# Layer 0's gate vector and layer 1's conditioning vectors moved from TensorE to GpSimd

## The reference

```
sc = jax.nn.silu(c)
scc = jax.nn.silu(c_ctx)
shift, scale, gate = jnp.split(sc @ mod_w[l] + mod_b[l], 3, axis=-1)
hx = modulate(rmsnorm(x, norm_g[l]), shift[:, None], scale[:, None])
...                                  # layer 0: convolution and two-way recurrence, layer 1: pooled mixer
x = x + gate[:, None] * out_x
```

## Time and profile before

| | |
|---|---|
| median of 3 runs (lowest to highest) | 1827.26 us (1826.8 to 1828.82) |
| profiled execution | 1828.44 us |
| its span in the profile | 1827.1 us |
| TensorE busy | 1749.3 us, 96% of the span |
| VectorE busy | 1059.6 us, 58% |
| ScalarE busy | 758.7 us, 42% |
| GpSimd busy | 18.9 us, 1% |
| mean granted TensorE clock | 0.976 of full speed |

### The profile page before, as it was taken

The page is one execution under the profiler, slowest core; times in us unless marked ns, Lnnn a source line. Parts: engine busy times, 40 slices in busy tenths (PEclk is TensorE's granted clock), DMA queues, the critical chain, the costliest instruction groups (busy, mean ns, idle before and its releaser), DMA issues.

```text
span 1827.1 us, 19870 instructions
## 1 busy us (share of the span) xinstructions
PE 1749.3 (96%) x8054; PEld 1411.2 (77%) x8054; DVE 1059.6 (58%) x1450; ACT 758.7 (42%) x1028; POOL 18.9 (1%) x39
## 2 busy tenths in 40 slices
PE   6899999999999999999889998999989999999996
PEld 4688888888778788888677865776778788888885
DVE  4766799899775756663455353444546644444333
ACT  3587654654442433333333544433433332322221
POOL 0000000000000000000000000000000000000000
PEclk9999999999898999999999998999999999999998
DMA  7344433333323232223222121222122222323321
GB/s 313 118 169 141 159 116 125 129 116 127 120 90 102 81 103 93 92 93 104 91 70 84 55 69 46 67 72 69 65 75 92 92 93 93 102 95 103 101 96 46
DMA packets 49963, 185.81 MB, mean 102 GB/s; under 512 B 5392, under 2 KB 5392, under 8 KB 49616
## 3 DMA queue, kind: packets, MB, share of 16 engines
q1 hardware_dynamic: 42624, 155.21, 25.2%
q0 software_dynamic: 4848, 17.80, 3.0%
q10 hardware_dynamic: 2400, 11.53, 1.6%
HBM read 182.42 MB, written 2.10 MB: 101 GB/s over the span
## 4 chain that ended last, share of the span: by engine, by line
PE 84%; DVE 7%; ACT 6%; issue 2%; ACTq 1%; DMA 0%; DVEq 0%
PE banks L1439 25%; PE banks L1441 24%; PE banks L1440 24%; PE banks L1471 2%; PE banks L1703 2%; ACT w_hi L389 1%; PE banks L1459 1%; PE banks L1452 1%; PE banks L1725 1%; PE banks L1747 1%; PE banks L1793 1%; DVE w_lo L816 1%; DVE u L950 1%; ACTq L415 1%; DVE h_lo L889 1%
## 5 line engine op out<-in xcount | busy, mean ns | idle before, releaser
L1439 PE MATMUL banks<-h_hi,w_hi 128*128 128x512 f32 x1408 | 559.3, 397 | 10.5 <-DVE h_lo L825 5.0
L1441 PE MATMUL banks<-h_hi,w_lo 128*128 128x512 f32 x1408 | 551.8, 392 | 0.0
L1440 PE MATMUL banks<-h_lo,w_hi 128*128 128x512 f32 x1408 | 551.4, 392 | 0.0
L816 DVE TENSOR_TENSOR w_lo<-raw,w_hi 128x1024 fp32r<-128x1024 f32 x292 | 355.4, 1223 | 290.1 <-ACT w_hi L389 289.8
L389 ACT ACTIVATE w_hi<-raw 128x1024 fp32r<-128x1024 f32 x292 | 304.2, 1051 | 153.9 <-PE banks L1441 142.5
L1439 PEld LDWEIGHTS banks<-h_hi,w_hi 128*128 128x128 f32 x1408 | 265.9, 189 | 79.1 <-issue 13.5
L1441 PEld LDWEIGHTS banks<-h_hi,w_lo 128*128 128x128 f32 x1408 | 266.2, 189 | 56.8
L1440 PEld LDWEIGHTS banks<-h_lo,w_hi 128*128 128x128 f32 x1408 | 266.5, 189 | 53.9 <-issue 0.7
L1011 DVE SCALAR_TENSOR_TENSOR U<-U,vec 128x512 f32<-128x512 f32 x112 | 83.3, 744 | 0.0
L1439 PE MATMUL banks<-y_hi,w_hi 128*128 128x512 f32 x192 | 76.9, 400 | 5.6 <-ACT gs L689 5.5
L1441 PE MATMUL banks<-y_hi,w_lo 128*128 128x512 f32 x192 | 75.7, 394 | 0.0
(11 more groups left out here) (349 smaller groups left out, 2283.9 us busy)
## 6 DMA issues: line engine op xcount, KB each, us to landing
raw<-weights SPq DMA_DIRECT2D x292, 512.0 KB, 3.2
mraw<-modw POOLq DMA_DIRECT2D x32, 512.0 KB, 4.0
mod<-modw ACTq DMA_DIRECT2D x4, 2048.0 KB, 23.1
X<-x_in ACTq DMA_DIRECT2D x1, 2048.0 KB, 13.5
out<-X SPq DMA_DIRECT2D x4, 512.0 KB, 2.7
ctx_x<-ctx_in ACTq DMA_DIRECT2D x1, 1024.0 KB, 19.8
cst<-consts POOLq DMA_DIRECT2D x1, 448.0 KB, 3.6
vec<-vecs POOLq DMA_DIRECT2D x1, 291.0 KB, 6.5
```

What stands on the lines that cost most here:

```text
L816: tt(slot(w_lo, c), slot(raw, c), slot(w_hi, c).bitcast(F32), ALU.subtract).then_inc(S["lo"], 1)
L1439: mm(o, wh, r_hi, start=start, stop=False)
L1440: mm(o, wh, r_lo, start=False, stop=False)
L1441: return mm(o, wl, r_hi, start=False, stop=stop)
```

## The change

The 32 late groups leave TensorE. The host lays their weights out transposed (`modt`: output in the partition, the 1024 inputs in the columns) and also gives `c` repeated in all 128 partitions (`crep`). ScalarE applies silu to it once (`csb`). GpSimd then works in 16 passes of two groups each: one transfer of 1 MB into the whole of `mraw`, one multiplication of both groups by `csb`, nine additions in place that each halve the width (from 1024 to 2), and a last addition that writes two columns of `modcol`. Every one of these instructions waits for the one before it, and the transfer of a pass waits for the end of the pass before. After pass 16 a semaphore `pm` tells VectorE, which adds the biases from `modcol` in one place, behind the main loop. The last four groups, formerly around the update of `X`, are ready there too. TensorE's wait in `yb` number 5 goes. Several semaphores for the later norms are merged; they order the same instructions as before. The descriptor scratch is set to 8192 bytes.

```
@@ pool()
-        for n in range(32):
-            if n >= MOD_RING:
-                e.wait_ge(S["mod_mm"], n - MOD_RING + 1)
-            e.dma_start(mod_slot(n), modw[16 + n, :, :]).then_inc(s_mraw[n % MOD_RING], 16)
+        e.dma_start(csb[:, :], crep).then_inc(S["crep"], 16)
+        own = Own(e, S["pmul"])
+        pair = mraw[:, :].rearrange("p (a n) -> p a n", a=2)
+        e.wait_ge(S["csb"], 1)
+        for n in range(16):
+            if n:
+                own.wait()
+            e.dma_start(pair, modt[2 * n:2 * n + 2, :, :].rearrange("a p n -> p a n")).then_inc(s_mraw[0], 16)
+            e.wait_ge(s_mraw[0], 16 * (n + 1))
+            own.did(e.tensor_tensor(pair, pair, csb[:, :].rearrange("p (a n) -> p a n", a=1).to_broadcast([P, 2, CW]), ALU.mult))
+            w = CW // 2
+            while w > 1:
+                own.wait()
+                own.did(e.tensor_tensor(pair[:, :, 0:w], pair[:, :, 0:w], pair[:, :, w:2 * w], ALU.add))
+                w //= 2
+            own.wait()
+            own.did(e.tensor_tensor(modcol[:, 2 * n:2 * n + 2].rearrange("p (a n) -> p a n", n=1), pair[:, :, 0:1], pair[:, :, 1:2], ALU.add))
+        own.wait()
+        e.tensor_copy(modcol[:, 32:33], modcol[:, 0:1]).then_inc(S["pm"], 1)
@@ act(), behind the two norms at the start
+        e.wait_ge(S["crep"], 16)
+        fn(csb[:, :], csb[:, :], ACT.Silu).then_inc(S["csb"], 1)
@@ dve(), behind the main loop
-        e.wait_ge(S["mod_mm"], 28)
-        bias_mod1(0, 20, 2)
-        bias_mod0(16, 24, 2).then_inc(S["mod_v"], 1)
+        e.wait_ge(S["pm"], 1)
+        own.did(tt(modv1, modcol[:, 8:32], cols("mod_b", 24, 24), ALU.add))
+        own.did(tt(modv0[:, 32:48:2], modcol[:, 0:8], cols("mod_b", 8, 16), ALU.add))
@@ dve(), in layer 1's norm
-        e.wait_ge(S["mod_mm"], 32)
-        bias_mod1(20, 24, BANK_OF[0])
@@ pe(): context loop, main loop, behind it, and around the update of X
-            mod_chunk(i, bank(2, 2, 2 * i))
-            mod_chunk(8 + 2 * i, bank(2, 2, 16 + 4 * i))
-            mod_chunk(9 + 2 * i, bank(2, 2, 18 + 4 * i))
-        for n in range(24, 28):
-            mod_chunk(n, bank(2, 2, 2 * n))
-            if f == 5:
-                e.wait_ge(S["mod_v"], 1)
-        e.wait_ge(S["res"], 1)
-        for n in (28, 29):
-            mod_chunk(n, bank(BANK_OF[0], 2, 2 * n))
-        for n in (30, 31):
-            mod_chunk(n, bank(BANK_OF[0], 2, 2 * n))
```

More of the change, by code:

```diff
@@ L120 @@
 SEMS = (
-    "vec x ctx cst cst2 out hi lo mm mod_mm v a zero eps pad sil sp_z sp_e wdt rows cols rows_c x_sum x_sq fsum f_sq "
+    "vec x ctx cst cst2 out hi lo mm crep csb pmul pm v a zero eps pad sil sp_z sp_e wdt rows cols rows_c x_sum x_sq fsum f_sq "
     "norm_t norm_hi norm_lo xp conv uhi ulo gread e2 mv sq thr scan sig uu "
-    "ushi uslo tgt sgb sgat sga cpe csum yact ybhi yblo mod_v ymu usum usq yln ysil yga yhi yalo res xsq xsum "
-    "lpad lcp dhi dsub dlo gsil gy gyhi gylo ores osq osum hsum "
+    "ushi uslo tgt sgb sgat sga cpe csum yact ybhi yblo ymu usum usq yln ysil yga yhi yalo res xsq xsum "
+    "lpad lcp dhi dsub dlo gsil gy gyhi gylo osq osum hsum "
     "bk4 bk5 bk6 bk7 ya_hi ya_lo yb_hi yb_lo yc_hi yc_lo yd_hi yd_lo ctap cact dtm dts dte dta "
@@ L166, in alternate, with program @@
         n += 1
-def program(nc, wts, modw, vecs, consts, x_in, ctx_in, out):
+def program(nc, wts, modw, modt, crep, vecs, consts, x_in, ctx_in, out):
     ctx = ExitStack()
@@ L240, in program @@
     csum = p("csum", T)
+    csb = p("csb", CW)
+    modcol = p("modcol", 33)
     u = p("u", T)
@@ L606, in act @@
             ahead("od", f, 1)
-            e.wait_ge(S["ores"], f + 1)
+            e.wait_ge(S["res"], NT + f + 1)
             if f > 1:
@@ L779, in act @@
             ahead("wo", f)
-            e.wait_ge(S["wres"], f + 1)
+            e.wait_ge(S["res"], 2 * NT + f + 1)
             if f > 1:
-                e.wait_ge(S["wsum"], f - 1)
-            fn(s1[:, :] if f == 0 else sqa[:, :], tile(X, f), ACT.Square).then_inc(S["wsq"], 1)
+                e.wait_ge(S["xsum"], NT - 1 + f - 1)
+            fn(s1[:, :] if f == 0 else sqa[:, :], tile(X, f), ACT.Square).then_inc(S["xsq"], 1)
             e.wait_ge(S["wg"], f + 1)
@@ L799, in act @@
                 ahead("fd", f, n)
-            e.wait_ge(S["fres"], f + 1)
+            e.wait_ge(S["res"], 3 * NT + f + 1)
             if f > 1:
-                e.wait_ge(S["fss"], f - 1)
-            fn(s1[:, :] if f == 0 else sqa[:, :], tile(X, f), ACT.Square).then_inc(S["fsq"], 1)
+                e.wait_ge(S["xsum"], 2 * (NT - 1) + f - 1)
+            fn(s1[:, :] if f == 0 else sqa[:, :], tile(X, f), ACT.Square).then_inc(S["xsq"], 1)
         sqrt_table()
@@ L870, in bias_mod0 @@
             return m
-        def bias_mod1(t0, t1, b):
-            own.did(tt(third(modv1[:, t0:t1]), bank(b, 2 * (t1 - t0), 16 + 2 * t0).rearrange("p (k two) -> p k two", two=2)[:, :, 0:1],
-                       third(cols("mod_b", t1 - t0, 24 + t0)), ALU.add))
         def norm_low(q, src, w, r, gain, shift, hi_t, lo_t, tmps):
@@ L1466, in mod_columns @@
             last.then_inc(S["cols"], 1)
[L1468 to L1471, removed]
-            last.then_inc(S["mod_mm"], 1)
         e.wait_ge(S["sil"], 1)
@@ L1613, in pe @@
             if f > 1:
-                e.wait_ge(S["ores"], f - 1)
+                e.wait_ge(S["res"], NT + f - 1)
             if f == 0:
@@ L1938, in lay_out @@
     assert weights.shape == (N_CHUNKS, P, CW), weights.shape
-    modw = np.concatenate([tiles_of(a["mod_w"][0]), tiles_of(a["mod_w"][1])])
+    modw = tiles_of(a["mod_w"][0])[:2 * NT]
+    modt = np.concatenate([a["mod_w"][0][:, 2 * D:], a["mod_w"][1]], 1).T.reshape(32, P, D)
+    crep = np.broadcast_to(a["c"].reshape(1, D), (P, D))
     f = lambda v: np.asarray(v).reshape(-1, P).T
@@ L1959, in lay_out @@
     xt = lambda x, t: np.ascontiguousarray(x[0].reshape(t, NT, P).transpose(2, 1, 0).reshape(P, NT * t))
-    return {"weights": weights, "modw": np.ascontiguousarray(modw), "vecs": vecs, "consts": constants(),
+    return {"weights": weights, "modw": np.ascontiguousarray(modw), "modt": np.ascontiguousarray(modt),
+            "crep": np.ascontiguousarray(crep), "vecs": vecs, "consts": constants(),
             "x_in": xt(a["x"], T), "ctx_in": xt(a["ctx"], TC)}
```

32 lines of the change are left out of this document (16 added, 16 removed).

## The result

The changed kernel takes 1909.35 us, median of 4 runs (1908.15 to 1911.03), beside 1828.04 for the kernel before in the same session: a ratio of 1.0444, 95% interval 1.0426 to 1.0462. It is 4.4% slower. The forecast was 1922, in a range of 1825 to 2000. The profiled execution has a span of 1906.9 us, 79.8 more than before.

A forecast was written before the change was run, and what follows sets the result against it. TensorE was taken as the bound, busy for 96% of the span. Start +3, context loop +10, main loop +92 and -4, behind it -4, around X -2: together +95 on 1828.4, 1923, median 1922; range 1825 to 2000.

The forecast's parts named there:

- That VectorE is held up by its two-input instructions alone: Beside GpSimd's arithmetic, VectorE's instructions with two SBUF inputs stand still, losing 90% of GpSimd's work to VectorE.
- GpSimd's work: Eleven instructions on 4094 columns a pass, at 2.50 ns a column plus 0.1 us each: 11.3 us, 181 in all.
- The pace of a pass: On GpSimd, 8.0 us transfer, 11.3 work and 7.9 turns for VectorE: 27.2 us a pass, sixteen passes ending at 511.
- Context passes: In the context loop VectorE becomes the bound at 18.3 us a pass instead of 17.0: +10 over eight passes.
- Main passes: In the main loop until 511, 5.9 passes of 49.6 us, each 15.6 longer: +92; the other 2.1 at 32: -4.
- The gain of taking groups from the main loop: Without two groups on TensorE, a main pass falls from 33.97 to 32 us, a gain of 2 a pass.
- the side by side case: Rival, chance 0.16: GpSimd and VectorE don't hold each other up; the kernel gets faster, 1795 us, between 1792 and 1811.
- a close thing: In the main loop TensorE is busy for all of 33.97 us and bounds it, with VectorE only 2.9 us behind.
- The start: ScalarE waits for crep before its first w_hi, and the pieces made behind that come late: +3 us, 1 to 7.
- Behind the main loop and around X: With the groups gone, sums start earlier: 4.2 us gained behind the main loop, 1.7 around the update of X.
- The slow GpSimd: Rival, chance 0.05: GpSimd needs over 3.3 ns a column, and the first sum passes 2000 us.
- The case with 6.55 ns: The same sum at GpSimd's highest rate per column: work 27.9 us, pass 43.8, context +79, main loop +260, total 2165.

The follow-up runs named there:

- e3: The changed kernel with each of GpSimd's arithmetic instructions turned into a memset of the same output: 1828.59 us, ratio 0.9999 to the kernel before.
- e4: The changed kernel with GpSimd's instructions on the weights turned into multiplications by a constant, one input instead of two: 1874.06 us, ratio 1.0249 to the kernel before.
- e1: The changed kernel with GpSimd keeping its sixteen 1 MB transfers but doing no arithmetic: 1825.96 us, ratio 0.999 to the kernel before.
- e6_pool_late: The kernel before with only the last eight groups on GpSimd, in four passes started after the main loop: 1855.92 us, ratio 1.0155.

## Why the prediction was right, and where it was wrong

The direction and the mechanism were right. The size, 1922 forecast and 1909 measured, came out partly by luck, since several terms were wrong and their errors nearly cancel. In the forecast's own terms, forecast and measured (by VectorE's scans and reciprocals): start +3, +5.1; context loop +10, +28.9; main loop +92 and -4, +54.7 and -2.0; behind it -6, -6.7; together +95, +80. By the steps:

- **That VectorE is held up by its two-input instructions alone: right.** L1055, and the unchanged L1036 and L960, show it; e3 and e4 show that it is GpSimd's reading. The forecast lost 90% of GpSimd's work to VectorE, 163 us. Measured, VectorE is busy 113.4 us longer than without arithmetic, of 235 us that GpSimd's instructions last: 48%, not 90%. Where the other half fell, into VectorE's idle time or its other instructions, the runs don't split.
- **GpSimd's work: 181 us forecast, 235 measured, 14.7 a pass instead of 11.3.** The rate of the multiplication was right in the mean (2.50 ns a column taken, 2.51 measured, 2.19 at best), but the additions are dearer: those of 2 to 64 columns in all take 0.34 to 0.59 us in the mean, where 0.1 and the columns were taken.
- **The pace of a pass: too slow.** 8.0 + 11.3 + 7.9 = 27.2 us were forecast. Passes start every 20.69 us in the context loop (transfers at 96.40 and 117.09). The 1 MB transfer lands in 5.4 us where twice 4.0 was taken, and the turns given to VectorE cost GpSimd far less than 7.9. So it was done at 418 us instead of 511.
- **Context passes: 18.3 forecast, 20.69 measured.** I divided VectorE's busy time by its share, as if only its sum counted. Its instructions are on the ring with ScalarE, so a blocked one lengthens the pass, and the pass came out as long as GpSimd's cycle, 20.69 both. By VectorE's second scan the gap to the kernel without arithmetic grows from 3.4 to 28.9 us over the loop.
- **Main passes: 49.6 forecast for six, measured 42.8, 50.7, 54.1 and 41.0 for four.** +55 us instead of +92, as GpSimd was done after four. The two errors partly cancel: forecast +102 for the two loops, measured +84.
- **The gain of taking groups from the main loop, 2 us a pass: wrong, it is 0.** The context loop's 1.7 a pass, counted in the side by side case, is 0 as well (e1). Only the first main pass gains 2.0 us, once. The step that failed is the first part's "a close thing" between TensorE and VectorE's busy time. I read "busy in all of it" as a bound. TensorE's records overlap and their ends are modelled: without its groups it is still recorded busy for 15.94 of 17.03 us, and 15.94 + 1.71 is more than the pass. The ring is in ScalarE's wait of 4.21 us for u_hi.
- **The start: 3 us forecast, 5.1 measured** (the first pair of scans, 87.60 before, 92.67 without arithmetic).
- **Behind the main loop and around X: -6 forecast, -6.7 in e1 and in the changed kernel. Right.**
- **The slow GpSimd: a slip in the sum.** By the forecast's own steps 3.3 ns a column gives about 1970, not 2000; it takes some 3.8 ns to pass 2000. The case with 6.55 ns adds up to 2161, not 2165. The forecast doesn't rest on either.
- **The clock falls in TensorE's waits: right, and it cost nothing that shows.** It is 0.80 in the pass of 54.10 us, where TensorE is recorded busy for 34.47; VectorE binds that pass with 53.59.
- **pm is ready in time: right.** modcol was done at 418, VectorE asked at 570.9.

## What to carry to other kernels

Before work goes to GpSimd, look at what VectorE does beside it: an instruction there with two SBUF inputs stopped here until a two-input GpSimd instruction had ended (1.7 us less beside a one-input one), and busy share is no measure of what that costs, since one blocked link in a chain moves everything behind it. Before work is taken from TensorE, look for the ring that repeats with the pass (who waits for whom, the same few microseconds each time), and don't take a full TensorE window for a bound; the cheap proof is a run with the work left out. And an engine's idle time can hold such work for nothing if its data are there: two more buffers gained 3 us here, where a whole engine lost 81. Look where such work is moved to as well: two groups beside the norm cost nothing, four held TensorE up.

## What the runs showed of the hardware that was not expected

- A one-input GpSimd instruction of 2048 columns lasts 5364 ns at least, a two-input one 4483. The Trainium skill (GPSIMD Engine Reference, "Engine selection") calls one-input work roughly line-rate there; this run doesn't bear that out. The 4497 ns of the Trainium skill (GPSIMD Engine Reference, "Performance versus the Vector engine") for a two-input addition agree with the 4483 ns of the shortest multiplication.
- Yet the one-input form costs less: 48 against 82 us. VectorE is let go before its end, which fits; no run separates it from other causes.
- A memset of 2048 columns lasts 1815 ns and disturbs nobody.
- A tanh behind the silu at the start needed no table load (1283 ns) of its own, but the exp behind it did; a silu put between a tanh and an exp (e6_pool_late) needed one itself and another behind it.
